# Up projection of a decoder trunk: three 256-column products per weight block into one half bank

## The reference, cut to what matters

```python
D_MODEL, SEQ, CONV_WIDTH, D_FF = 2048, 256, 3, 5632

def conv_ffn(h, w_up, conv_w, conv_b, w_down):
    u = h @ w_up                                   # (256, 2048) @ (2048, 11264)
    up = jnp.pad(u, ((0, 0), (CONV_WIDTH - 1, 0), (0, 0)))
    u = conv_b + conv_w[0] * up[:, 0:S] + conv_w[1] * up[:, 1:S + 1] + conv_w[2] * up[:, 2:S + 2]
    g, val = u[..., :D_FF], u[..., D_FF:]
    return (jax.nn.silu(g) * val).astype(h.dtype) @ w_down
```

## Time and profile before

| | |
|---|---|
| median of 3 runs | 2505.92 us (2504.85 to 2506.89) |
| the profiled execution | 2505.45 us, of which its span is 2503.6 us |
| TensorE busy | 2483.4 us, 99% of the span, 12502 matmuls |
| weight loads busy | 2094.7 us, 84% |
| VectorE busy | 1560.2 us, 62% |
| ScalarE busy | 1276.0 us, 51% |
| mean granted TensorE clock | 0.999 of full speed |

### The profile page before, as it was taken

One profiled execution on the slowest core, in us unless ns is written; L12 is line 12 of the kernel. 1 busy time (PEld: TensorE's weight loads), 2 busy tenths in 40 slices (PEclk: granted clock), 3 DMA queues, 4 the chain that ended last, 5 costly groups with the idle time before them and its releaser, 6 DMA issues.

```text
span 2503.6 us, 35035 instructions
## 1 busy us (share of the span) xinstructions
PE 2483.4 (99%) x12502; PEld 2094.7 (84%) x12502; DVE 1560.2 (62%) x2173; ACT 1276.0 (51%) x1845; POOL 34.1 (1%) x92
## 2 busy tenths in 40 slices
PE   8999999999999999999999999999999999999998
PEld 7888888888888888888888888888888888888887
DVE  5555665677767677544564446566777776775444
ACT  6444554665555555434454455556655555554443
POOL 0000000000000000000000000000000000000000
PEclk9999999999999999999999999999999999999999
DMA  7656455556556665666566564455566566656665
GB/s 238 191 183 198 159 159 177 174 170 194 180 182 189 188 181 184 214 198 198 181 203 187 176 194 138 163 173 177 172 183 197 174 190 185 192 178 213 193 189 168
DMA packets 243113, 462.04 MB, mean 185 GB/s; under 512 B 17032, under 2 KB 19016, under 8 KB 243016
## 3 DMA queue, kind: packets, MB, share of 16 engines
q1 hardware_dynamic: 237384, 450.27, 57.6%
q10 hardware_dynamic: 5632, 10.49, 1.3%
HBM read 458.60 MB, written 2.10 MB: 184 GB/s over the span
## 4 chain that ended last, share of the span: by engine, by line
PE 95%; DVE 2%; ACT 1%; DMA 1%; issue 0%; POOL 0%; DVEq 0%; SPq 0%; POOLq 0%; ACTq 0%
PE acc L1421 18%; PE acc L1423 18%; PE acc L1422 18%; PE acc L1447 12%; PE acc L1444 6%; PE aux L1447 6%; PE tp L1447 6%; PE aux L1444 3%; PE tp L1444 3%; DVE w_lo L858 1%; PE tp L1455 1%; PE tp L1630 1%; PE acc L1443 1%; PE acc L1655 1%; ACT w_hi L435 0%
## 5 line engine op out<-in xcount | busy, mean ns | idle before, releaser
L858 DVE TENSOR_TENSOR w_lo<-raw,w_hi 128x1024 fp32r<-128x1024 f32 x848 | 1022.7, 1222 | 699.2 <-ACT w_hi L435 697.8
L435 ACT ACTIVATE w_hi<-raw 128x1024 fp32r<-128x1024 f32 x848 | 869.0, 1054 | 440.7 <-PE acc L1423 370.6
L1421 PE MATMUL acc<-w_hi,a_hl 128*128 128x512 f32 x1216 | 484.2, 398 | 4.2 <-DVE a_hl L885 4.0
L1423 PE MATMUL acc<-w_hi,a_hl 128*128 128x512 f32 x1216 | 475.4, 391 | 0.0
L1422 PE MATMUL acc<-w_lo,a_hl 128*128 128x512 f32 x1216 | 474.5, 390 | 0.0
L1447 PE MATMUL acc<-a_hl,w_hi 128*128 128x512 f32 x1260 | 473.1, 398 | 0.0
L1444 PE MATMUL acc<-a_hl,w_lo 128*128 128x256 f32 x1344 | 377.6, 281 | 0.0
L1447 PEld LDWEIGHTS acc<-a_hl,w_hi 128*128 128x128 f32 x1260 | 236.7, 188 | 56.5
L1421 PE MATMUL acc<-w_hi,hid_hi 128*128 128x512 f32 x704 | 274.0, 389 | 0.0
L1423 PE MATMUL acc<-w_hi,hid_lo 128*128 128x512 f32 x704 | 273.9, 389 | 0.0
L1422 PE MATMUL acc<-w_lo,hid_hi 128*128 128x512 f32 x704 | 273.9, 389 | 0.0
(11 more groups left out here) (200 smaller groups left out, 2234.6 us busy)
## 6 DMA issues: line engine op xcount, KB each, us to landing
raw<-in_w_up SPq DMA_DIRECT2D x352, 512.0 KB, 3.9
raw<-in_w_down SPq DMA_DIRECT2D x176, 512.0 KB, 4.6
raw<-in_w_in_ab SPq DMA_DIRECT2D x96, 512.0 KB, 4.2
raw<-in_w_in_c SPq DMA_DIRECT2D x96, 512.0 KB, 4.4
raw<-in_w_out_ab SPq DMA_DIRECT2D x32, 512.0 KB, 4.7
raw<-in_w_out_c SPq DMA_DIRECT2D x32, 512.0 KB, 4.6
raw<-in_w_mk SPq DMA_DIRECT2D x16, 512.0 KB, 4.0
raw<-in_w_mq SPq DMA_DIRECT2D x16, 512.0 KB, 4.0
```

What stands on the lines that cost most here:

```text
L435: act.activation(w_hi[:, s], raw[:, s], ACT.Copy).then_inc(hi_ready, 1)
L858: dve.tensor_tensor(w_lo[:, s], raw[:, s], w_hi[:, s].bitcast(F32), ALU.subtract).then_inc(lo_ready, 1)
L1421: pe.matmul(o, hi[:, kt, rows], w_hi[:, slot, j, :], start=(kt == 0), stop=False)
L1423: last = pe.matmul(o, lo[:, kt, rows], w_hi[:, slot, j, :], start=False, stop=(kt == kts - 1))
```

## The change

`slab_turned` loops over the three products first and over the four blocks inside: for each `kt`, hi by hi for the four blocks, hi by lo for the four, lo by hi for the four. Each product streams 256 columns, and all add into the first half of the block's bank. The second halves are not used any more. `u_copy` and `u_add` are gone. `u_scale` moves up to `q` 0 or 8 and reads PSUM itself, in two instructions that multiply by `rstd_row`. The waits for the buffer (`tap_a`, `conv_done`) and for the last slab move from ScalarE to VectorE with it. `u_free` waits for `u_done` in place of `u_sum`.

```diff
-        def u_half(par, k, b):
-            at = slice(b * SEQ, (b + 1) * SEQ)
-            return acc[:, par, :, at] if k == 0 else (tp, aux)[par][:, :, at]
+        def u_half(par, k):
+            return acc[:, par, :, 0:SEQ] if k == 0 else (tp, aux)[par][:, :, 0:SEQ]
...
-                def u_copy(G, dst, par):
-                    act.wait_ge(slab_used, G * GS + (n0 + PHASE["up"] + GS))
-                    if not (isinstance(G, int) and G < 2):
-                        act.wait_ge(*LV(L, "conv_done", (G - 1) * 8))
-                    for k in range(2):
-                        act.activation(dst[:, 2 * k:2 * k + 2, :], u_half(par, k, 1), ACT.Copy)\
-                            .then_inc(LS(L, "u_cp"), 1)
...
-                def u_add(G, dst, par):
-                    for k in range(2):
-                        d = dst[:, 2 * k:2 * k + 2, :]
-                        dve.wait_ge(*LV(L, "u_cp", G * 2 + (k - 1)))
-                        dve.tensor_tensor(d, u_half(par, k, 0), d, ALU.add).then_inc(LS(L, "u_sum"), 1)
-                def u_scale(G, dst):
-                    dve.wait_ge(*LV(L, "u_sum", G * 2))
+                def u_scale(G, dst, par):
+                    dve.wait_ge(slab_used, G * GS + (n0 + PHASE["up"] + GS))
                     if isinstance(G, int) and G == 1:
                         dve.wait_ge(*LV(L, "row_st", 1))
-                    dve.tensor_tensor(dst[:], dst[:], rstd_row[:].to_broadcast([P, 4, SEQ]), ALU.mult)\
-                        .then_inc(LS(L, "u_done"), 1)
+                    if not (isinstance(G, int) and G < 2):
+                        dve.wait_ge(*LV(L, "tap_a", (G - 1) * 4))
+                        dve.wait_ge(*LV(L, "conv_done", (G - 1) * 8))
+                    for k in range(2):
+                        dve.tensor_tensor(dst[:, 2 * k:2 * k + 2, :], u_half(par, k),
+                                          rstd_row[:].to_broadcast([P, 2, SEQ]), ALU.mult).then_inc(LS(L, "u_done"), 1)
...
-                    for f, bank in enumerate(u_banks(par)):
-                        cols = slice(f * P, (f + 1) * P)
-                        both = a_hl[:, kt].rearrange("p a b -> p (a b)")
-                        if kt == 0:
-                            pe.matmul(bank, w_hi[:, slot, j, cols], both, start=True, stop=False)
-                        last = pe.matmul(bank[:, SEQ:2 * SEQ], w_lo[:, slot, j, cols], a_hi[:, kt, :],
-                                         start=False, stop=False)
-                        if kt:
-                            last = pe.matmul(bank, w_hi[:, slot, j, cols], both,
-                                             start=False, stop=(kt == KT - 1))
+                    for k, (w, x) in enumerate(((w_hi, a_hi), (w_hi, a_lo), (w_lo, a_hi))):
+                        for f, bank in enumerate(u_banks(par)):
+                            last = pe.matmul(bank[:, 0:SEQ], w[:, slot, j, f * P:(f + 1) * P], x[:, kt, :],
+                                             start=(kt == 0 and k == 0), stop=(kt == KT - 1 and k == 2))
...
                     elif not (isinstance(G, int) and G < 2):
-                        pe.wait_ge(*LV(L, "u_sum", (G - 2) * 2))
+                        pe.wait_ge(*LV(L, "u_done", (G - 2) * 2))
```

More of the change, by code:

```diff
@@ L219, in build @@
             mo_hi=4, mo_lo=4, mv_half=1,
-            u_t=1, u_ev_a=1, u_ev_d=1, row_mm=1, row_st=1, u_cp=42, u_sum=42, u_done=21, tap_a=88, conv_done=176, silu=11, prod=11, hid_hi=11, hid_lo=11)
+            u_t=1, u_ev_a=1, u_ev_d=1, row_mm=1, row_st=1, u_done=42, tap_a=88, conv_done=176, silu=11, prod=11, hid_hi=11, hid_lo=11)
         def LS(layer, name):
@@ L788, in conv_tap @@
                     else:
-                        act.wait_ge(*LV(L, "u_done", G))
+                        act.wait_ge(*LV(L, "u_done", G * 2))
                     if not (isinstance(i, int) and i == 0):
@@ L808, in val_tail @@
                 def val_tail(i, q):
-                    if q == 0:
-                        u_copy(i * 2 + 1, u_val, 1)
                     if q == 3:
@@ L824, in up_pair @@
                                 u_evac()
-                            else:
-                                u_copy(i * 2, u_gate, 0)
                         if q == GS + (4 if first else 3):
@@ L843, in _ @@
                             if s in (8, 9):
-                                act.wait_ge(*LV(L, "u_done", 2 * FF_GROUPS - 1))
+                                act.wait_ge(*LV(L, "u_done", 2 * (2 * FF_GROUPS - 1)))
                                 gain_chunk(ffn, s - 8)
@@ L1290, in val_tail @@
                 def val_tail(i, q):
[L1291 to L1294, removed]
+                    if q == 0:
+                        u_scale(i * 2 + 1, u_val, 1)
                     if q == 3:
@@ L1314, in up_pair @@
                                 u_evac()
-                        if q == GS + 1:
-                            if first:
-                                row_store()
-                            else:
-                                u_add(i * 2, u_gate, 0)
-                        if q == GS + 2 and not first:
-                            u_scale(i * 2, u_gate)
+                            else:
+                                u_scale(i * 2, u_gate, 0)
+                        if first and q == GS + 1:
+                            row_store()
                         if q == GS + (4 if first else 3):
```

## The result

| | before | after |
|---|---|---|
| median | 2505.57 us (4 runs, 2504.85 to 2506.89) | **2524.89 us** (4 runs, 2523.49 to 2525.94) |
| profiled execution, span | 2505.45 us, 2503.6 us | 2524.44 us, 2522.6 us |
| matmuls | 12502 | 15190 |

The ratio is 1.0075, with a 95% interval from 1.0062 to 1.0088. The change makes the kernel slower by 19.3 us. The forecast was 2517 us.

The account below looks back on a forecast made before the run. TensorE, busy for 99% of the span, was taken to bound the kernel. The profiled 2505.45 us plus 11.8 us for slower matmul slots, and nothing for evacuation or waits, made 2517 us; range 2496 to 2555 us.

Parts of the forecast that it names:

- What bounds the kernel: Whole kernel: TensorE, busy 99% of the span; only its work, a new wait of it or its clock changes the time.
- one slot: Turned up projection: start to start time of a 256-column matmul with a fresh 128 by 128 weight block; 0.119 us taken.
- its one term: Turned up projection: three slots of 0.119 us make 0.357, 0.0044 above the old pair; 2688 blocks give +11.8 us.
- The 0.1175: Slot in us averaged over two neighbouring 256-column matmuls where `kt` 0 ends, which together take 0.24 and 0.23 us.
- The row with the right neighbour: Where `kt` 0 ends: second of two neighbouring 256-column matmuls, preceded by one of its kind; 0.12 us at both places.
- The lower bound: Turned matmuls: half of the 512-column slot of 0.2271 us, 0.1136 us, the stream's pace without loss; 32 us gained.
- The reason for the rise: Turned matmuls: a weight load takes about 0.11 us, hidden under 512 columns but with nothing to spare under 256.
- The upper rival: Turned matmuls: the load sets the pace, 0.1255 us a slot, 64 us lost, 2570 us; chance 0.13.
- the pair: Old up projection: one 512-column and one 256-column matmul per block, 768 columns, costing 0.3526 us.
- The two rules of the Trainium skill: Turned matmuls: one rule's N / 2.4 + 2.5 ns would gain 67 us; the other's 60 cycles per matmul lose 67 us.
- The evacuation: Group ends: copies and additions removed, VectorE falls from 2.58 to 1.38 us per group; beside TensorE's work, nothing gained.
- VectorE's wait: Group ends: VectorE waits for the last slab before preparing slab n + 2, 2.7 us in time; starving TensorE had chance 0.02.

Follow-up runs that it names:

- evac: Kernel before with the change's 256-column matmuls, except each group's first contraction tile, which keeps its 512-column product; copies and additions stay as before: 2523.71 us, ratio 1.0072.
- narrow16: Changed kernel with only 16 of the 128 weight columns in each turned matmul, same streams and count: 2471.85 us, a slot of 0.1135 us.
- the narrow runs: Changed kernel with fewer of the 128 weight columns in each turned matmul: 16 gave 2471.85 us, 96 gave 2492.60 us.
- forder16: Changed kernel with its two inner loops exchanged, so a block's three products follow one another into one bank, and 16 weight columns: 2472.70 us, a slot of 0.1136 us.

## Why the prediction was right or wrong, point by point

- **What bounds the kernel: right.** TensorE's busy time, its groups without idle time and evac show that only TensorE's work moved the time.
- **That all hangs on one slot: right.** 2688 blocks, 8.1 us per ns, and the slot measured 0.120.
- **The sum: its one term was mis-sized.** I put 0.119 us, +11.8 us; 0.120 us gives +19.9, and 19.0 were measured in the profiled executions. The change costs 1.6 times what was forecast. The step that failed is the mean between 0.1175 and 0.12. The 0.1175 took in a matmul whose predecessor was a 512-column one, which the earlier trace rows show as 0.11 in one place; the changed kernel has none such within the stage. The row with the right neighbour had said 0.12 all along, at both places.
- **The lower bound: a reading that failed.** Half of the 0.2271 us of the earlier trace rows was called the pace of the stream if nothing is lost per matmul. But that slot holds a loss of 0.013 us too, and half of it is no pace of anything. That narrow16 comes to 0.1135 is a coincidence: its loss of 0.007 us is about half of 0.013.
- **The reason for the rise: half right.** The slot does depend on the width of the weights, as the narrow runs show. But by the prediction the cost appears only where the stream is too short to cover the load, and that is wrong. "Under a 512-column matmul this load is hidden twice over" doesn't hold: the same 0.013 us beside the columns is lost there. One more matmul with its load per block is +0.013 us, and the end of the alternation gives back 0.006: together the +0.007 that was measured. The forecast came near without the right reason, because its slot was read from rows; the credit for 2517 us is the earlier trace rows's, not the mechanism's.
- **The upper rival: fell.** It put all of the pair's excess on the 256-column matmul, 0.1255 us. In the pair the 256-column matmul takes 0.117 us and the wide one 0.236, so most of the excess lies on the wide one. The pair's 0.3526 us are 0.320 of columns and 0.0326 beside them: 0.0133 for each of the two matmuls, the wide one too, and 0.006 for the alternation.
- **The two rules of the Trainium skill.** Its page "TensorE: Matmul & The Clock Gate", section "Back-to-back issue gap", gives N / 2.4 + 2.5 ns for a lone gap: N / 2.4 is the slope that the runs show, but in these streams the constant is 13 ns with 128-column loads and 7 ns with 16. Its page "TensorEngine Tiling (Array Packing)", section "Instruction Overhead", gives about 60 cycles for each matmul: taken as an addition, as the prediction took it, a fixed cost does speak against the change, but the runs show 13 ns, half of the 25 estimated.
- **The evacuation: worth nothing, right.** The copies that went held 50.1 us of ScalarE, and VectorE's groups of the evacuation fell from 108.3 to 57.6 us, both as forecast. The engines' busy time fell by less, 24.9 us and 39.9 us. Busy time counts overlapping instructions once, and fewer overlap now: the 848 `w_hi` copies rose from 869.0 to 889.7 us on ScalarE, while their durations add up to 893.8 us before (848 x 1054 ns) and 895.5 after.
- **VectorE's wait: harmless, right.** The margin is 2.9 us where 2.7 was forecast.

## What to carry to other kernels

Count the matmuls with their loads, not only the columns: on a saturated TensorE each fp32r matmul with a 128-column load cost about 13 ns beside its columns here, so a 512-column matmul should not be cut in two to spare work on engines that nobody waits for. Where wide and narrow streams must both be there, put them in runs of their own kind; alternating them cost 6 ns a pair here, and undoing most of it gave 0.5% for a change of two loops. When a slot has to be read for a new pattern, take the row whose predecessor is of the right kind, and don't average it with the others.

## What the runs showed of the hardware that I had not expected

- The cost beside the columns doesn't vanish under a long stream: 13 ns per matmul at 256, 384 and 512 columns with 128 columns of weights. At 256 columns it is 9 ns with 96 and 7 ns with 16.
- With 192 columns and 128 columns of weights the slot is 0.112 us, 0.018 above stream and loss. If that floor is the load's, it reaches up to some 235 columns, an estimate.
- After a run of 256-column matmuls the first pairs of 512-column ones take 0.47 and 0.46 us instead of 0.45, and the order of matmuls with the same operands and counts is worth 13.6 us.
- The 48 matmuls of the earlier trace rows take 0.1170 us with 16-column weights, and those of narrow16 and forder16 0.1135 and 0.1136. The bank isn't the reason; what is wasn't tried.
